# Gate and up matrices of each routed expert loaded whole instead of in two halves, in a two-layer MoE decoder on one core

## What is computed

```python
N_EXPERTS = 64; TOP_K = 8; D_MODEL = 1024; D_EXPERT = 256; SEQ = 256; DEPTH = 2

def swiglu(x, w_gate, w_up, w_down):
    return (jax.nn.silu(x @ w_gate) * (x @ w_up)) @ w_down

for l in range(DEPTH):
    ...
    x = layer_norm(DEEPNORM_ALPHA * x + g1 * mixed, ln1_g[l], ln1_b[l])
    h = x * (1.0 + sc2) + sh2
    ffn = (swiglu(h, w_sh_gate[l], w_sh_up[l], w_sh_down[l])
           + routed_moe(h, w_router[l], router_bias[l], w_exp_gate[l], w_exp_up[l], w_exp_down[l]))
    x = layer_norm(DEEPNORM_ALPHA * x + g2 * ffn, ln2_g[l], ln2_b[l])
```

## Time and profile before

| what | value |
|---|---|
| median of 3 runs | 1551.06 us (1548.32 to 1552.45) |
| the profiled execution | span 1544.6 us from its first to its last instruction; the page gives no other time of it |
| PE busy | 1398.7 us, 91% of the span |
| DMA queue q1 | 497.24 MB, 85.2% of the 16 DMA engines' span |
| read from HBM | 496.11 MB, 322 GB/s over the span |
| blocks of the expert part | 60, in 48 rounds |
| mean granted clock of PE | 0.959 |

### The profile page before, as it was taken

How to read it: one execution, slowest core, us unless ns; L and a number is a source line. 1 busy time by engine, 2 the same in 40 slices (tenths; PEclk the granted TensorE clock), 3 DMA queues, 4 the chain that set the end, 5 groups by cost and what they waited for, 6 DMA issues and landing times.

```text
span 1544.6 us, 25815 instructions
## 1 busy us (share of the span) xinstructions
PE 1398.7 (91%) x7809; PEld 740.9 (48%) x7810; DVE 491.4 (32%) x1091; ACT 178.8 (12%) x367; POOL 153.0 (10%) x453
## 2 busy tenths in 40 slices
PE   2989899999999999988789989999999999989884
PEld 0465554555455445534247465454554455445442
DVE  1524622222222222222553462222322222212225
ACT  0133100000000001000023210000000000000000
POOL 0001011111111111111000101111111111111110
PEclk9899799999999999999899979999999999999997
DMA  9976859998999989999788656094999998999992
GB/s 353 355 284 235 354 196 353 353 367 330 377 326 381 332 344 347 405 397 409 281 338 323 239 211 237 21 358 175 358 356 359 343 365 335 382 396 401 404 409 101
DMA packets 129926, 497.70 MB, mean 322 GB/s; under 512 B 15048, under 2 KB 15056, under 8 KB 123232
## 3 DMA queue, kind: packets, MB, share of 16 engines
q1 hardware_dynamic: 129888, 497.24, 85.2%
HBM read 496.11 MB, written 1.08 MB: 322 GB/s over the span
## 4 chain that ended last, share of the span: by engine, by line
PE 81%; DVE 7%; issue 5%; DMA 3%; ACT 2%; SPq 1%; DVEq 0%; ACTq 0%
PE ps L789 28%; PE ps L805 14%; PE ps L746 12%; PE ps L823 7%; PE ps L685 4%; DMA ring<-in_w_ada 3%; PE ps L755 3%; PE ps L711 2%; DVE w L1292 2%; PE ps L798 2%; PE ps L555 2%; ACT w L937 2%; PE ps L619 1%; PE ps L738 1%; PE ps L703 1%
## 5 line engine op out<-in xcount | busy, mean ns | idle before, releaser
L789 PE MATMUL ps<-ring,w 128*64 128x512 f32 (+1 forms) x2432 | 435.4, 613 | 41.4 <-issue 39.9
L789 PEld LDWEIGHTS ps<-ring,w 128*64 128x64 f32 (+1 forms) x2432 | 138.6, 128 | 307.3 <-issue 307.2
L746 PEld LDWEIGHTS ps<-w 128*128 128x128 f32 x1984 | 235.7, 191 | 99.2 <-issue 99.2
L746 PE MATMUL ps<-w 128*128 128x128 f32 x1984 | 263.8, 281 | 0.0
L805 PE MATMUL ps<-ring,w 128*32 128x512 f32 (+1 forms) x1216 | 232.0, 602 | 0.0
L1292 DVE SCALAR_TENSOR_TENSOR w<-ps,w 128x256 f32<-128x256 f32 x60 | 29.0, 484 | 420.8 <-ACT w L937 420.8
L1280 DVE CAST scat<-ps 128x512 fp32r<-128x512 f32 x120 | 83.0, 692 | 201.8 <-PE ps L805 201.8
L925 ACT ACTIVATE w<-ps 128x512 f32<-128x512 f32 x124 | 74.1, 597 | 515.2 <-PE ps L746 515.2
L823 PE MATMUL ps<-scat 128*128 128x512 f32 x480 | 125.0, 402 | 0.0
L1271 DVE TENSOR_SCALAR w<-ps 32x1 f32<-32x1 f32 x248 | 55.7, 225 | 178.1 <-PE ps L823 156.2
L805 PEld LDWEIGHTS ps<-ring,w 128*32 128x32 f32 (+1 forms) x1216 | 56.0, 124 | 84.5 <-issue 69.4
(11 more groups left out here) (210 smaller groups left out, 810.3 us busy)
## 6 DMA issues: line engine op xcount, KB each, us to landing
ring<-in_w_exp_gate SPq DMA_DIRECT2D x256, 512.0 KB, 8.2
ring<-in_w_exp_up SPq DMA_DIRECT2D x256, 512.0 KB, 9.4
ring<-in_w_exp_down SPq DMA_DIRECT2D x128, 1024.0 KB, 10.2
ring<-in_w_ada SPq DMA_DIRECT2D x48, 1024.0 KB, 8.3
w<-in_w_out SPq DMA_DIRECT2D x2, 4096.0 KB, 16.1
w<-in_w_in SPq DMA_DIRECT2D x2, 3840.0 KB, 18.9
rows<-mod_rows SPq DMA_DIRECT2D x8, 512.0 KB, 3.9
w<-in_w_uq SPq DMA_DIRECT2D x2, 1728.0 KB, 12.3
```

The costliest lines, as they stand in the source:

```text
L746: last = mm(ps[:, B_0 + half, (kt % 4) * P:(kt % 4 + 1) * P], h2p[:, j, kt * P:(kt + 1) * P], S[:, j, :], start=j == 0, stop=j == NT - 1)
L789: last = mm(ps[unit * g:unit * g + unit, B_F, :].rearrange("p (q f) -> p q f", q=2), hTb[:, kt, unit * g:unit * g + unit], gate_up(k)[:, : ...
```

## The change

A gate or up matrix is loaded by one transfer of 1 MB, 8 KB on each partition. The semaphore `gu_half_done`, the wait for it in `refill`, the wait of PE in the middle of a block and the second set of `gu_landed` semaphores are gone. All of a pair's gate and up matrices are issued after `gu_done`, and PE waits for all of them ahead of the round.

```diff
-            def load_gate_up(l, half, slots, experts):
-
-                kts = slice(half * KT // 2, (half + 1) * KT // 2)
+            def load_gate_up(l, slots, experts):
+
                 for slot, e in zip(slots, experts):
                     for dst, w in ((gate_w, w_exp_gate), (up_w, w_exp_up)):
                         src = w[ds(l, 1), ds(e, 1)].rearrange("a b (p k) f -> p (a b k) f", k=KT)
-                        sp.dma_start(dst(slot)[:, kts, :], src[:, kts, :]).then_inc(gu_landed[half][slot // 2], 16)
+                        sp.dma_start(dst(slot), src).then_inc(gu_landed[slot // 2], 16)
...
                     slots = (2 * q, 2 * q + 1)
-                    sp.wait_ge(s["gu_half_done"], used)
-                    passed(sp)
-                    load_gate_up(l, 0, slots, experts)
                     sp.wait_ge(s["gu_done"], used)
                     passed(sp)
-                    load_gate_up(l, 1, slots, experts)
+                    load_gate_up(l, slots, experts)
                     sp.wait_ge(s["down_done"], used * 2)
                     passed(sp)
                     load_down(l, slots, experts)
...
                         for q in halves:
-                            pe.wait_ge(gu_landed[0][q], loads * 64)
+                            pe.wait_ge(gu_landed[q], loads * 64)
...
                             for kt in range(KT):
-                                if kt == KT // 2:
-                                    last.then_inc(s["gu_half_done"], 1)
-                                    for q in halves:
-                                        pe.wait_ge(gu_landed[1][q], loads * 64)
-                                    passed(pe)
                                 for g, k in enumerate(slots):
```

More of the change, by code:

```diff
@@ L323, in decoder_trunk @@
         shsil_ready shmid_ready sel_ready sh_gate_done rank_done table_ready rg_ready
-        sh_landed gu_half_done S_ready gath_done hT_ready gu_done sil_ready mid_ready midT_done midT_ready down_done
+        sh_landed S_ready gath_done hT_ready gu_done sil_ready mid_ready midT_done midT_ready down_done
         ST_done ST_ready y0_ready y1_ready scat_done sh_free out_done ang_ready hi_ready y_free count_ready key_ready place_ready order_done gc_ready rc_ready pro_link
@@ L329, in decoder_trunk @@
         ada_used = [sem(f"ada_used{i}") for i in range(ADA_BUFS)]
-        gu_landed = [[sem(f"gu_landed{half}_{i}") for i in range(RING // 2)] for half in range(2)]
+        gu_landed = [sem(f"gu_landed{i}") for i in range(RING // 2)]
         down_landed = [sem(f"down_landed{i}") for i in range(RING // 2)]
@@ L453, in _ @@
                 sp.dma_start(rbias, lay(router_bias, l).to_broadcast([P, E])).then_inc(s["rbias_in"], 16)
-                for half in range(2):
-                    load_gate_up(l, half, (0, 1), (0, 1))
+                load_gate_up(l, (0, 1), (0, 1))
                 load_down(l, (0, 1), (0, 1))
@@ L460, in _ @@
                 sp.dma_start(down_w(3), lay(w_sh_down, l).rearrange("a (k p) d -> p (a k) d", p=P)).then_inc(s["sh_landed"], 16)
-                for half in range(2):
-                    load_gate_up(l, half, (2,), (2,))
+                load_gate_up(l, (2,), (2,))
                 load_down(l, (2,), (2,))
@@ L473, in _ @@
                 passed(sp)
-                for half in range(2):
-                    load_gate_up(l, half, (3,), (3,))
+                load_gate_up(l, (3,), (3,))
                 sp.wait_ge(s["sh_free"], l + 2)
@@ L513, in _ @@
             tr = nc.tensor.transpose
-            start_counts(pe, "gu_half_done gu_done midT_done ST_done scat_done", "gath_done down_done",
+            start_counts(pe, "gu_done midT_done ST_done scat_done", "gath_done down_done",
                          [s["sh_free"], *ada_used])
```

## The result

| kernel | median | runs | ratio to before, 95% interval |
|---|---|---|---|
| before | 1549.69 us | 1546.62 to 1552.45 (4) | |
| changed | 1634.82 us | 1632.56 to 1639.74 (4) | 1.0566 [1.0545, 1.0586] |

The change costs 85 us, where 57 were forecast. The median itself, 1634.8 us, lies just inside the forecast range (1584 to 1636). Taken as a ratio, 1.0566 on the 1551.06 us that stood ahead of the prediction is 1638.9 us, just above its upper end.

A forecast was written before the change was run, and what follows sets the result against it. PE bounds eleven periods and the DMA queue five; waits of 22.6 and 13.9 us, DMA-bound periods 21.1 and layer ends -0.2 sum to +57.4 us, so 1551.1 becomes 1608.5 us, range 1584 to 1636.

The forecast's parts named there:

- eleven PE-bound quad rounds: Quad rounds ending PE-bound periods: PE has 10.7 us of other work, needs 12.75, so waits 2.05 us each, 22.6 in all.
- the block behind them: Pair 0, released by the quad round and needed 11.2 us later: waits 1.55 us at nine places, 13.9 us.
- the DMA-bound periods: Five periods at the ends of the layers' expert parts: 66.8 us each, 64.7 for a layer's first, together +21.1 us.
- the queue is dry there: In each DMA-bound period the DMA queue runs dry for some 4 to 7 us around the quad round's products.
- Pair 0's refill for a quad round: In PE-bound periods this refill has a whole block more of time and stays hidden, adding nothing.
- the price of the transfers: Refill of a pair's four gate and up matrices on an idle queue: usable 12.4 us after the first issue.
- four w_ada tiles at 779.42: Tiles of the same size and packet shape, issued on an idle queue, from which the 12.4 us refill was estimated.
- the step from landing to PE's start: In each refill, 12.5 us from issue to PE's start; with 0.25 us before issue, 12.75 from gu_done to start.
- the products behind the new waits: Gate and up products of PE-bound quad rounds were taken to stay at 7.1 us, with no clock cost in the sum.
- The clock falls too: Rival: new 2 us waits before eleven quad rounds cost PE its clock, 23 us more, 1632 us; chance 0.17.
- the distance of 6.5 us between span and median: Median of the runs lies 6.5 us above the profiled span; kept when turning 1602 us into 1608.5 us.
- The rule on large transfers: Skill advice to batch to 1 MiB or more; as a fee per transfer it would save 2 us for every matrix.

The follow-up runs named there:

- e10: e8 with the gates too issued only behind gu_done, PE still starting on the gates alone: 1551.03 us, ratio 1.0023.
- e11: e8 with early release of the gates kept, but PE waiting for gates and ups ahead of a round: 1564.51 us, ratio 1.0111.
- e4: The changed kernel with two extra unused matmuls on PE ahead of the gate and up wait in the quad round and round 0: 1619.05 us, ratio 1.047.
- e3: The changed kernel's release and wait, but each gate or up matrix in two 512 KB transfers with 4 KB packets: 1734.31 us, ratio 1.1218.
- e8: The kernel before, split by matrix: whole gates, then whole ups, each released and waited for apart, all gate products before up products: 1540.66 us, ratio 0.9948.
- e2: The kernel before with halves issued early as before, but PE waiting for both halves ahead of a round: 1615.89 us, ratio 1.0436.
- e6: The changed kernel with each matrix still one 1 MB transfer but in 4 KB packets, output not the reference's: 1636.31 us, ratio 1.0581.

## Why the prediction was right and wrong

**Right: the mechanism and its places.** The eleven PE-bound quad rounds wait (2.45 us more than before on average, 2.05 forecast), the block behind them too (2.0 us more than before, 1.55 forecast), the DMA-bound periods grow, and the queue is dry there, for 5 to 8 us in each (4 to 7 forecast). Pair 0's refill for a quad round stays hidden: the other blocks begin 17.8 us apart, as before. e10 and e11 show the same from the other side: with whole matrices the PE-bound periods do not move when only one of the waits is late.

**Right: the price of the transfers.** Four matrices were taken from four w_ada tiles at 779.42. In the changed kernel SP makes the first issue of the refill behind 642.25 at 649.65, and the chain has its last transfer landed at 651.13 + 10.90 = 662.03: 12.4 us.

**Mis-sized: the step from landing to PE's start.** I took 12.5 us from issue to start, 0.1 beyond the 12.4. PE starts at 662.52, 0.5 us behind the landing, and SP issues 0.3 and not 0.25 us behind the products. From release to start that is 13.4 us in the refill shown, 13.2 on average, for 12.75. At the PE-bound places this is 8.6 us, and it is part of the DMA-bound difference.

**Failed: the products behind the new waits, kept at 7.1 us.** The sum put the clock's part in them at nothing; it measured 15.0 us. "The clock falls too" was a rival, and it is what happened. I gave it 0.17 and 1632 us, against 0.65 for the forecast, on the grounds that 2 us is short beside 7 and that PE is full on both sides. The trace of before had a place that speaks against the first ground, and I had not looked for it. It is in the w_ada products between the layers; timeline of PE, and windows ahead of and behind it (columns as the earlier trace rows):

```profile
764.03 1.06 PE L529 MATMUL ps<-ring,c 128*32 128x512 f32 x8 [1.66 <-DMA ring<-in_w_ada]
767.61 1.94 PE L529 MATMUL ps<-ring,c 128*32 128x512 f32 x8 [2.52 <-DMA ring<-in_w_ada]
```

```profile
760.60:767.20 6.60, 2.83 (x28) 0.46 (x16) 6.24 (x10) 0.29 (x1) 0.00 (x0) 1.00 0.96 351
767.40:774.00 6.60, 5.32 (x24) 0.69 (x24) 1.58 (x2) 0.00 (x0) 0.00 (x0) 0.50 0.61 258
```

Across an idle time of 2.52 us the grant went from 1.00 to 0.50 (2.4 to 1.2 GHz). The place is not quite alike: another idle time, of 1.66 us, lay just ahead, and PE was busy for only 2.83 of the 6.60 us before, so it leaves the second ground, the full PE, standing. The changed kernel does not: there PE is busy up to the wait, and nine of eleven PE-bound quad rounds run their products in 8.65 to 8.77 us. e4 shows that the wait is the cause: with it filled, none does, and the kernel is 16 us faster. Why two rounds kept their clock behind waits of 2.3 and 2.4 us stays open.

That rival as I worked it out, 23 us, was too dear: each drop cost 1.7 and not 2.1 us, and two rounds kept their clock. That its 1632 lies so near the measured 1634.8 is partly luck, since the other 18 us by which the forecast fell short are not in it, and the distance of 6.5 us between span and median, which is, was not there.

**The DMA-bound periods** came to +29.0 for +21.1 us. The first of each layer, forecast 64.7, took 65.5 and 67.3 (the latter behind a quad round that had lost its clock); the other three, forecast 66.8, took 68.1 to 68.7, with quad products of 9.2 to 9.9 us ahead of them (9.2 forecast), and the later start on top. These two account for 0.5 to 1.2 us of the 1.3 to 1.9 by which each passed the forecast; what the rest is, no run shows.

**The rule on large transfers.** The prediction set the Trainium skill's advice to batch to 1 MiB (DMA: Bandwidth & Descriptors, Bandwidth) aside, since in a full queue halves ran at 412 GB/s. The runs show each to be half of the matter. In the comparison with equal waits, larger transfers are worth 99 us (e3 to changed), most of it in the PE-bound periods, where each refill starts on an empty or nearly empty queue. e8, with whole matrices and the other order of products, is 6 us below the kernel before. What the change lost it lost by the waits that came with the size. I had read only the full queue, at the earlier trace rows, and not the filling one. The 2.0 us beside the bytes, which the prediction takes from the same page of the Trainium skill, are there a fit for transfers issued by GpSimd; this kernel's are issued by SP, and no term of the sum rests on that figure.

## What to carry to other kernels

In this kernel splitting a transfer was worth something only through the waits that it lets move, one for the release of the old data and one for the use of the new; write down, for each, the time from release to need and the time of the refill, and do not give up both. Where both large transfers and a split are wanted, split along what is already stored in one piece (here gate and up), and let the compute order follow. And price a short idle time of the matmul engine with the clock it may cost, also if it is only 2 us.

## What the runs showed of the hardware

- Idle PE of 2.3 to 2.6 us was followed by products at the lower clock (8.65 to 8.77 us for 7.07) in nine of eleven quad rounds, and of 0.5 to 0.9 us in none of eleven (e4). Such a wait does not always cost the clock: of 14 waits of 2.3 to 2.6 us ahead of blocks of two slots, ten left it at its upper level, and in e2 two quad rounds kept it behind 2.3 and 2.8 us.
- A burst of eight 512 KB transfers on a nearly empty queue moved 277 GB/s with the DMA engines at a busy share of 1.00; four of 1 MB moved 418 to 425, with packets of 8 KB or of 4 KB. The busy share alone does not tell a slow queue from a full one. Whether the number or the size of the transfers does it stays open. Packets of 4 KB alone cost about 7 us (e6, less the block that it has not).
- Transfers of 8 KB packets to 64 of the 128 partitions moved 224 GB/s at a busy share of 1.03, about half.
- Matmuls of 256 columns with twice as many weight loads cost PE 0.04 us a block more than those of 512 columns (7.11 to 7.13 us for 7.07 to 7.09).
